# Router logits in four column groups of TensorE, with the sum over the groups in the transposing matmul

## What is computed

```python
def ec_ffn(h, w_router, w1, w3, w2):
    b, n, d = h.shape
    cap = EC_CAPACITY * n // N_EXPERTS
    logits = jnp.einsum('bnd,de->bne', h, w_router).astype(jnp.float32)
    aff = jax.nn.softmax(logits, axis=-1).transpose(0, 2, 1)
    gate, idx = lax.top_k(aff, cap)
    xs = jax.vmap(lambda hb, ib: hb[ib])(h, idx)
    ...
```

## Time and profile before

| | us |
|---|---|
| median of three runs | 1707.56 |
| lowest, highest | 1706.84, 1709.25 |
| span of the profiled execution | 1704.8 |
| PE busy in it | 1608.4 (94%) |
| DVE busy | 521.3 (31%) |
| ACT busy | 434.5 (25%) |
| POOL busy | 110.6 (6%) |

### The profile page before, as it was taken

One profiled execution on the slowest core, in us unless ns is written; L12 is line 12 of the kernel. 1 busy time (PEld: TensorE's weight loads), 2 busy tenths in 40 slices (PEclk: granted clock), 3 DMA queues, 4 the chain that ended last, 5 costly groups with the idle time before them and its releaser, 6 DMA issues.

```text
span 1704.8 us, 26703 instructions
## 1 busy us (share of the span) xinstructions
PE 1608.4 (94%) x10868; PEld 1264.2 (74%) x10868; DVE 521.3 (31%) x1182; ACT 434.5 (25%) x1010; POOL 110.6 (6%) x112
## 2 busy tenths in 40 slices
PE   4899998999999999999938999999999999999997
PEld 2745544665666656544428999999999999999996
DVE  3101433563635545113781111111111111111114
ACT  4200111553545535243320111111111111111114
POOL 0005300000000000021101000000000000000000
PEclk9899999999999999999958999999999999999998
DMA  8760004000000000062136778777788787777865
GB/s 328 284 275 29 0 0 149 14 1 14 0 0 13 0 2 1 1 233 88 62 124 235 273 264 303 275 268 269 278 288 290 262 309 267 274 265 277 295 222 235
DMA packets 113650, 288.31 MB, mean 169 GB/s; under 512 B 10111, under 2 KB 15142, under 8 KB 110398
## 3 DMA queue, kind: packets, MB, share of 16 engines
q1 hardware_dynamic: 108846, 270.27, 43.1%
q0 software_dynamic: 4752, 17.30, 3.8%
HBM read 265.39 MB, written 21.64 MB: 168 GB/s over the span
## 4 chain that ended last, share of the span: by engine, by line
PE 61%; issue 31%; DMA 3%; DVE 2%; POOL 1%; ACT 1%; SPq 0%; POOLq 0%; DVEq 0%; ACTq 0%
PE ps L920 30%; PE ps L938 15%; PE ps L492 8%; PE ps L554 2%; DMA wreg<-in_x_sample_dram 1%; POOL wreg L1713 1%; PE ps L505 1%; PE ps L585 1%; PE ps L895 1%; PE ps L903 1%; DMA mreg<-in_x_prompt_dram 1%; PE ps L574 1%; PE ps L545 1%; DVE list_idx L1485 0%; DMA wreg<-in_w_ada_dram 0%
## 5 line engine op out<-in xcount | busy, mean ns | idle before, releaser
L920 PE MATMUL ps<-mreg,wreg 128*128 128x144 f32 x4096 | 517.6, 287 | 0.0
L920 PEld LDWEIGHTS ps<-mreg,wreg 128*128 128x128 f32 x4096 | 510.2, 191 | 0.2 <-issue 0.2
L938 PE MATMUL ps<-mreg,wreg 128*128 128x144 f32 x2048 | 265.3, 286 | 0.0
L938 PEld LDWEIGHTS ps<-mreg,wreg 128*128 128x128 f32 x2048 | 257.7, 190 | 0.0
L1625 DVE TENSOR_TENSOR mreg<-ps,mreg 128x144 f32<-128x144 f32 x128 | 39.4, 308 | 475.6 <-PE ps L920 475.6
L665 PE MATMUL ps<-wreg 128*128 128x512 f32 (+2 forms) x400 | 174.2, 525 | 0.0
L1160 ACT ACTIVATE mreg<-ps 128x144 f32<-128x144 f32 x128 | 37.3, 291 | 442.7 <-PE ps L920 442.7
L1063 ACT ACTIVATE hreg<-ps 128x512 f32<-128x512 f32 (+2 forms) x200 | 103.2, 516 | 167.4 <-PE ps L696 167.1
L696 PEld LDWEIGHTS ps<-const,hreg 128*128 128x128 f32 x648 | 76.6, 140 | 92.4 <-ACT hreg L1063 67.4
L492 PE MATMUL ps<-hreg,wreg 128*128 128x512 f32 (+1 forms) x432 | 143.2, 489 | 0.0
L765 PE MATMUL ps<-wreg,mreg 128*128 128x512 f32 x288 | 128.5, 597 | 1.1 <-DVE wreg L1422 1.1
(11 more groups left out here) (208 smaller groups left out, 1186.8 us busy)
## 6 DMA issues: line engine op xcount, KB each, us to landing
wreg<-in_w_e_dram SPq DMA_DIRECT2D x96, 2048.0 KB, 12.0
wreg<-in_w_ada_dram SPq DMA_DIRECT2D x24, 1024.0 KB, 10.2
out_dram<-wreg SPq DMA_DIRECT2D x9, 512.0 KB, 2.6
mreg<-in_x_sample_dram SPq DMA_DIRECT2D x8, 512.0 KB, 6.8
wreg<-in_w_out_dram SPq DMA_DIRECT2D x1, 4096.0 KB, 13.4
wreg<-in_x_sample_dram SPq DMA_DIRECT2D x8, 512.0 KB, 7.0
x_rows<-wreg SPq DMA_DIRECT2D x8, 512.0 KB, 2.9
xn_rows<-wreg SPq DMA_DIRECT2D x8, 512.0 KB, 2.7
```

The lines of the kernel that those rows point to most:

```text
L920: mm = pe.matmul(o[:, 0:CAP], w[s][:, k, (f % 4) * P:(f % 4 + 1) * P], xsT[b][:, k, :], start=(k == 0), stop=(k == KD - 1))
L938: mm = pe.matmul(bank[4 + dm % 2][:, 0:CAP], w2[f // 4][:, f % 4, dm * P:(dm + 1) * P], hidT[:, f, :], start=(f == 0), stop=(f == 7))
```

## The change

The eight feature blocks of a tile are split over four column groups: group q takes blocks 2q and 2q + 1, accumulates them over two rounds, and writes its partial sums of 16 experts to partitions 32q to 32q + 15 of bank 6. For that `w_r` has 32 columns a block, of which the last 16 are zero (a new memset; the load waits for `cleared`). The eviction takes all 128 partitions. `by_token` is no longer a transpose but a matmul with `quad_sum`, a 128 x 16 matrix with a one where the partition is 32q + e and the column e: it turns the logits to tokens and adds the four partial sums at once. `quad_sum` is reduced from the identity on DVE, ahead of the first gated eviction.

```diff
-        w_r = sb("w_r", [P, KD, NE])
+        w_r = sb("w_r", [P, KD, 32])
+        quad_sum = sb("quad_sum", [P, NE])
...
-            sp.dma_start(w_r[:], w_router[0].rearrange("(k p) e -> p k e", p=P)).then_inc(w_r_in, 16)
+            sp.wait_ge(cleared, 1)
+            sp.dma_start(w_r[:, :, 0:NE], w_router[0].rearrange("(k p) e -> p k e", p=P)).then_inc(w_r_in, 16)
...
-                for k in range(KD):
-                    mm = pe.matmul(bank[6][0:NE, 0:P], w_r[:, k, :],
-                                   h2T[:, k, t * P:(t + 1) * P], start=(k == 0), stop=(k == KD - 1))
+                for r in range(2):
+                    for q in range(4):
+                        k = 2 * q + r
+                        mm = pe.matmul(bank[6][32 * q:32 * q + 32, 0:P], w_r[:, k, :],
+                                       h2T[:, k, t * P:(t + 1) * P], start=(r == 0), stop=(r == 1))
...
-                    mm = pe.transpose(bank[7][:, t * NE:(t + 1) * NE], aff[0:NE, t * P:(t + 1) * P], ident[0:NE, 0:NE])
+                    mm = pe.matmul(bank[7][:, t * NE:(t + 1) * NE], aff[:, t * P:(t + 1) * P], quad_sum[:],
+                                   start=True, stop=True)
...
             dve.memset(w_pool_sb[:], 0.0)
+            dve.memset(w_r[:], 0.0)
             dve.memset(b_rows, 0.0).then_inc(cleared, 1)
...
-                dve.tensor_copy(aff[0:NE, t * P:(t + 1) * P], bank[6][0:NE, 0:P]).then_inc(lg_out, 1)
+                dve.tensor_copy(aff[:, t * P:(t + 1) * P], bank[6][:, 0:P]).then_inc(lg_out, 1)
...
             dve.wait_ge(gain_ok, 2)
+            dve.tensor_reduce(quad_sum[:], ident.rearrange("p (q e) -> p e q", q=4)[:, 0:NE, :], AX_X, ALU.add)
             dve.wait_ge(flip_in, 16)
```

## The result

The changed kernel takes **1698.93 us** (median of 4 runs, 1697.33 to 1700.78) against 1707.2 for the kernel before on the same chip (4 runs, 1706.31 to 1709.25): a ratio of 0.995, 95% interval 0.9938 to 0.9962. Its profiled execution spans 1695.4 us, before it was 1704.8. Predicted were 1699.6, with a range of 1697.2 to 1703.2.

What follows compares the result with a forecast made beforehand. PE was taken as the bound up to 850.7 us, DVE's written order next in the second half. First half -4.2, second -3.43, tail -0.28 sum to -7.9 us; from the median 1707.56 that gives 1699.6, range 1697.2 to 1703.2.

Steps and rivals of the forecast that it cites:

- Rivals 1 and 2: DVE loses its gain to other waits (1702.4, chance 0.12); only two column groups run at once (1701.4, chance 0.08).
- Four at a time: Logits on PE: four column groups run in the time of one, 0.67 us a tile for 1.92, saving 1.25.
- rival 2: Logits: passes of one group must follow one another, eight slots, 1.09 us a tile, saving 0.83; 1701.4, chance 0.08.
- rival 5: Logits: no weight load runs under another group's matmul, 3.5 us a tile; 1724.6 in all, chance 0.04.
- `by_token`: Logits to tokens on PE: eight records at 0.12 us replace 0.35, +0.6 us for each group of four tiles.
- upper bound of +2.9: Token matmuls of four tiles with load and matmul one after the other, 8 x 0.41 - 0.35 us.
- `quad_sum`: Head of the stage: the reduction on DVE delays PE's first gated eviction, +0.22 us, nothing if the stores' landing hides it.
- Who is late in the second half: From 794.2 to 850.7: PE saves 5.0 us, but DVE's own order then bounds; -3.5 from four waits, -3.43 in all.
- the rival in which DVE gives its gain back: Second half: DVE stops sooner for ACT or GpSimd, keeping about 1.0 us of gain; 1702.4, chance 0.12.
- The link by way of `h2_turn(7)`: Second half: PE and the ACT copy it needs both reach 835.1, so even, 0.1 us at most.
- Tail: After the second half: DVE's 0.57 wait for tile 8's logits goes, its `by_token(2)` wait grows 0.25; net -0.28 us.
- Experts: Expert stage to the end: no change, 0 us; wrong if they start at a granted clock that costs more.

Runs made afterwards that it cites:

- one-group kernel: Changed kernel with all eight feature blocks of a tile in one column group of 32, the rest of the change kept: 1708.82 us, ratio 1.0003.
- by doubling: Changed kernel with every token matmul issued twice into the same place: 1741.87 us, ratio 1.0216.
- two-group kernel: Changed kernel with two column groups of 32 instead of four, four blocks each: 1701.99 us, ratio 0.9967.

## Why the prediction was right

The time came 0.7 us below the forecast; the sum of the stretches is 1.4 larger than the sum of terms, since the stretches all came out a little shorter than forecast. Rivals 1 and 2, at 1702.4 and 1701.4, lie in the stated range too. The interval of the ratio ends at 1700.7, so the time alone speaks against them by little; the traces decide. Point by point:

- **Four at a time.** Held, with the size (0.67 forecast, 0.65 measured, and 4 x 1.28 from the one-group kernel). The row of L505, with 512 moving columns and in another stage, gave the right answer for 128. Two groups at a time, rival 2, would be 1.07 a tile, and the kernel made that way is 3.7 us slower; the rival that nothing overlaps, 3.5 us a tile, is out, and with it, here, the rule of the Trainium skill (TensorE: Matmul & The Clock Gate, Part 3: Packing small matmuls) that a weight load overlaps with matmuls in flight only where the row group differs: these four groups use the same 128 rows, and the busy time fell from 19.1 to 6.2 us, 3.1 times. Even one group, the same rows for all sixteen records, takes 1.93 us and not the 3.5 that rival 5 counted for loads and passes in turn. The part's other figure, 2.38 times for three column groups, was scaled to some 3.2 for four in the prediction, an estimate; 3.1 lies near it.
- **Where the stage's marks stand.** The first `probs_out` copy is at 789.35 (forecast 790.0), the last gated eviction at 841.94 (843).
- **`by_token`.** +0.6 a group was too high: 0.82 - 0.35 = +0.47 on the records, and less on the stretches: the one-group kernel, which has the new token matmuls and the old logits, is 0.40 and 0.41 longer there than the kernel before. The pace was mis-sized, 0.112 a record (by doubling) for 0.12; the rest stays open. The upper bound of +2.9 is excluded.
- **`quad_sum`.** +0.22 forecast; PE's wait grew by 0.17, the stretch by 0.08. DVE's row overlaps its neighbours: 0.16 between its start and the next one's.
- **Who is late in the second half.** Right in its mechanism, and 0.5 too cautious. All four waits went to nothing, 0.99 + 0.23 + 0.51 + 1.85 = 3.58, rounded down to 3.5 in the sum; a wait of 0.20 before the eviction of tile 5's second half (797.20 before), which the sum left out, went too. `by_token(1)`'s wait became 1.16 (1.19 forecast, 1.12 before), and that of `probs_out` behind it fell from 1.46 (at 848.90 before) to 1.35. These make -3.58 - 0.20 + 0.04 - 0.11 = -3.85; the last 0.08 is not resolved. DVE's three waits of 1.69 for ACT did not grow, so the rival in which DVE gives its gain back fell. The two-group kernel shows how near the two engines are: of PE's last 1.68 only 0.86 arrives.
- **The link by way of `h2_turn(7)`.** Forecast even, and it starts at 830.23 without a bracket, 7.37 earlier than before, of which 4.8 were gained ahead of the second half. One wait was not foreseen: the logits of tile 7 wait 0.42 for the copy of tile 6's, since both use bank 6. DVE asks for them at 835.6, so it costs nothing. The idle time that was forecast for PE ahead of `by_token(1)` and `h2_turn(7)` is hardly to be seen: 0.56 us of the second stretch in all.
- **Tail.** -0.39 for -0.28. The 0.57 went, and DVE's wait for the token matmuls grew by 0.37 (0.33, at 867.11 before, to 0.70), where 0.25 was taken for one slow slot; the other 0.19 is not resolved.
- **Experts.** Taken at nothing, and nothing came (-0.28). But the reason was incomplete: the prediction asked about the clock with which they start, not about TensorE's code. The change itself adds 18 instructions ahead of the loop, two per token matmul. With 36 more, as in the run with nine matmuls ahead of the loop, it ends 38 us slower than the kernel before instead of 8 faster. That it stayed clear of this was luck: the place of the loop stood in no term. This was a rival that the prediction should have had, with a place and a price.

## What to carry to other kernels

When a matmul has few stationary columns, splitting its contraction over column groups and letting a later matmul add the parts can cost that later matmul little (0.4 us for four tiles here, against 5.1 gained); look for a form with column groups elsewhere in the trace, and take its pace. Before summing a gain on one engine, go through the other engine's idle brackets in the same stretch: what they hold is about the most that can arrive (3.8 held, 3.9 arrived here), and two versions with half the step show the hand-over. And when a kernel has a long loop, compare the packets of the instruction queue before and after any edit ahead of it.

## What the runs showed that was not expected

**The place of a loop's code is worth up to 49 us here.** 36 instructions more shortly ahead of the expert loop, most of them in time in which TensorE stood idle, made six jumps back cost 5.0 us each and the clock fall behind each; 16 or 256 more, or 36 behind the loop, cost nothing (92, 38, 39 and 38 packets). The Trainium skill (Runtime: NRT & Kernel Launch, Instruction fetch mechanics) states that instructions come in blocks of 16 KiB, 256 instructions, read in sequence, that TensorE has room for 2048, and that a taken branch to a block that isn't held stalls until it is fetched. The runs agree with the block (0.62 MB in 38 packets, and a shift of 256 that changes nothing) and with the stall. The page also calls the window two pages; no run agrees with that, since the loop of 6.5 packets jumps back in the changed kernel with no stop and no fetch. Room for 2048, the page's figure, would hold a turn of 1665 wherever it begins, in seven packets or in eight. That eight are too many, and that nine come in at each stopped jump, would follow if TensorE reads one packet ahead of the turn's end; no run here shows that.

**A wait of 2.58 us where 1.25 stood cost another 1.6 us of clock.** The granted mean was 0.85 and 0.81 over ten us, 0.57 in the worst four, and came back to 1.00 while PE worked without a break.
